# Two-layer decoder kernel: the memory norm's factors per token, and a new order of five Vector steps

## The reference

```python
def first_block(...):
    h = h + short_conv_mixer(rms_norm(h, a_norm), ...)
    h = h + swiglu(rms_norm(h, f_norm[0]), f_w_gu[0], f_w_down[0])
    k_cmp, v_cmp, k_slc, v_slc, k_win, v_win = shared_kv(h, kv_norm, w_kv, ...)
    h = h + nsa_mixer(rms_norm(h, b_norm), b_w_qg, b_w_o, k_cmp, ...)
    h = h + swiglu(rms_norm(h, f_norm[1]), f_w_gu[1], f_w_down[1])
    return rms_norm(h, final_norm)              # eps 1e-5

def second_block(x, c, ...):
    mod = silu(c) @ w_ada + b_ada               # six vectors of 1024
    h = modulate(rms_norm_2(x, g_mix), sh_m, sc_m)   # eps 1e-6
    x = x + gt_m * token_mixer(h, ...)
    h = modulate(rms_norm_2(x, g_ffn), sh_f, sc_f)
    return x + gt_f * swiglu_2(h, ...)
```

## Time and profile before

| | |
|---|---|
| median of 3 runs | 971.0 us (970.72 to 971.22) |
| profiled execution, its own time | 971.74 us |
| its span | 970.0 us |
| TensorE busy | 954.0 us, 98% |
| Vector busy | 712.9 us, 73% |
| Scalar busy | 488.6 us, 50% |
| POOL busy | 88.0 us, 9% |
| mean granted TensorE clock | 0.996 of full |
| chain that ended last | TensorE 86%, Vector 8%, Scalar 3%, issue 2%, DMA 1% |
| DMA | 186.99 MB, 193 GB/s |

### The profile page before, as it was taken

One profiled execution on the slowest core, in us unless ns is written; L12 is line 12 of the kernel. 1 busy time (PEld: TensorE's weight loads), 2 busy tenths in 40 slices (PEclk: granted clock), 3 DMA queues, 4 the chain that ended last, 5 costly groups with the idle time before them and its releaser, 6 DMA issues.

```text
span 970.0 us, 19340 instructions
## 1 busy us (share of the span) xinstructions
PE 954.0 (98%) x7854; PEld 919.1 (95%) x7854; DVE 712.9 (73%) x1131; ACT 488.6 (50%) x712; POOL 88.0 (9%) x132
## 2 busy tenths in 40 slices
PE   8999999999999999899999999999999999999998
PEld 8999999999999977589999999999999999999998
DVE  5886877777769878968777777698876676565654
ACT  5444644433447557847444433537667555334441
POOL 7000000000000042420000000020000000000000
PEclk9999999999999999999999999999999999999999
DMA  9846848686845762038486868435354357564611
GB/s 265 270 174 217 287 157 301 229 285 199 285 165 161 238 217 89 1 133 298 150 299 229 293 204 286 145 113 181 101 173 150 108 179 258 175 218 134 232 66 44
DMA packets 131533, 186.99 MB, mean 193 GB/s; under 512 B 6289, under 2 KB 102929, under 8 KB 131473
## 3 DMA queue, kind: packets, MB, share of 16 engines
q1 hardware_dynamic: 123984, 159.69, 49.7%
q0 software_dynamic: 6912, 25.17, 7.4%
q10 hardware_dynamic: 576, 1.29, 0.4%
HBM read 185.09 MB, written 1.05 MB: 192 GB/s over the span
## 4 chain that ended last, share of the span: by engine, by line
PE 86%; DVE 8%; ACT 3%; issue 2%; DMA 1%; POOL 1%; DVEq 0%; SPq 0%; ACTq 0%; POOLq 0%
PE ps L1898 43%; PE ps L1976 19%; PE ps L1894 12%; PE ps L1896 4%; DVE g_lo L1174 1%; ACT g_hi L668 1%; DMA g_raw<-in_w_up 1%; PE ps L1946 1%; PE ps L2095 1%; PE ps L2042 1%; DVE rstd L1230 1%; PE ps L2160 1%; DVE ybuf L1194 1%; PE ps L2175 1%; DVE e_even L1541 1%
## 5 line engine op out<-in xcount | busy, mean ns | idle before, releaser
L1898 PE MATMUL ps<-opa_hi,g_hi 128*128 128x256 f32 x864 | 230.1, 287 | 1.3 <-ACT opa_hi L717 1.1
L1898 PE MATMUL ps<-opa_lo,g_hi 128*128 128x256 f32 x864 | 220.8, 283 | 0.0
L1898 PE MATMUL ps<-opa_hi,g_lo 128*128 128x256 f32 x864 | 182.8, 284 | 0.0
L1292 DVE TENSOR_TENSOR g_lo<-g_raw,g_hi 128x2048 fp32r<-128x2048 f32 x54 | 123.8, 2293 | 69.0 <-ACT g_hi L742 69.0
L1898 PEld LDWEIGHTS ps<-opa_hi,g_hi 128*128 128x128 f32 x864 | 166.5, 193 | 4.6 <-issue 4.1
L1898 PEld LDWEIGHTS ps<-opa_lo,g_hi 128*128 128x128 f32 x864 | 162.4, 192 | 0.1
L1976 PE MATMUL ps<-hid_hi,d_hi 128*128 128x256 f32 x528 | 147.8, 280 | 1.8 <-DVE hid_lo L1295 1.7
L1976 PE MATMUL ps<-hid_hi,d_lo 128*128 128x256 f32 x528 | 147.5, 279 | 0.0
L1976 PE MATMUL ps<-hid_lo,d_hi 128*128 128x256 f32 x528 | 147.4, 279 | 0.0
L1174 DVE TENSOR_TENSOR g_lo<-g_raw,g_hi 128x2048 fp32r<-128x2048 f32 x54 | 123.6, 2289 | 30.9 <-ACT g_hi L668 30.5
L1898 PEld LDWEIGHTS ps<-opa_hi,g_lo 128*128 128x128 f32 x864 | 139.8, 193 | 0.0
(11 more groups left out here) (340 smaller groups left out, 1809.4 us busy)
## 6 DMA issues: line engine op xcount, KB each, us to landing
g_raw<-in_f_w_gu SPq DMA_DIRECT2D x44, 1024.0 KB, 8.7
ada_raw<-in_w_ada POOLq DMA_DIRECT2D x48, 512.0 KB, 6.3
d_raw<-in_f_w_down SPq DMA_DIRECT2D x22, 1024.0 KB, 5.1
g_raw<-in_w_in SPq DMA_DIRECT2D x14, 1024.0 KB, 8.3
g_raw<-in_w_gate SPq DMA_DIRECT2D x11, 1024.0 KB, 7.2
g_raw<-in_w_up SPq DMA_DIRECT2D x11, 1024.0 KB, 9.7
d_raw<-in_w_down SPq DMA_DIRECT2D x11, 1024.0 KB, 5.3
g_raw<-in_a_w_in SPq DMA_DIRECT2D x10, 1024.0 KB, 8.3
```

The source lines that it names most:

```text
L1292: dve.tensor_tensor(part_view(g_lo, g0 + r, True), raw_cols(c % 2, r % 2, True), part_view(g_hi, g0 + r, True).bitcast(F32), ALU.subtract) ...
L1898: mm = pe.matmul(pair(b)[:, a, :], wt[:, a * P:(a + 1) * P], xt, **st)
```

## The change

The memory norm's two sums come from one set of products with the squares as weights and `sum_w` (two columns per channel tile: g^2 + 1e-6, and 1) moving. The result has tokens on partitions: two columns for each half of the tokens, in banks 4 and 5. Scalar takes two roots of 128x2, Vector the reciprocals of them, and scales the identity by each token's factor (`diag`, 128x128, one for each half). TensorE multiplies `ones` by it (`spread`), which gives the factor of each token on all partitions, in PSUM. `norm_parts` reads the fused factor from there; Scalar copies the plain one to `rstd` later. Vector's sums of squares go; the split of step `MX + 1` is done in two halves, one of them ahead of the reciprocals. POOL makes `sum_w` for `gain_sq`. The counts of the patterns move to bank 3. Outside the norm: the split of the second down slice goes behind the hidden split of step 0 (feed-forward 0 and 1), the scaling of `gmod` and `q_gain` behind step 3, and the two accumulation pairs behind the splits in steps 0 and 1 of the key/value products.

```diff
--- before.py
+++ after.py
@@ -147,8 +147,10 @@
     qg_lo = sb("qg_lo", [P, KT, 48], F32R, on=over_q)
     over_q.close()
     over_q = ExitStack()
-    gain_sq = sb("gain_sq", [P, KT, P], on=over_q)
-    sb("pad_q", [P, 3 * KT * 48 - KT * P], on=over_q)
+    sum_w = sb("sum_w", [P, KT, 2], on=over_q)
+    r_cols = sb("r_cols", [P, 2, TT], on=over_q)
+    diag = sb("diag", [P, 2, TT, P], on=over_q)
+    sb("pad_q", [P, 3 * KT * 48 - 2 * KT - 2 * TT - 2 * TT * P], on=over_q)
     ctx.push(over_q)
     if_raw = sb("if_raw", [P, KT, 8])
     if_hi = sb("if_hi", [P, KT, 36], F32R)
...
@@ -629,10 +631,10 @@
                 pool.tensor_scalar(bias_h[:, h % 2, :], dist[:, :], SLOPES[h], None, ALU.mult).then_inc(bias_made, 1)
         if last_stage >= 5:
 
-            for k in range(KT):
-                g = par_col("final_norm", k)
-                const(pool.tensor_scalar(gain_sq[:, k, :], ones[:, :], g, g, ALU.mult, ALU.mult))
-            const(pool.tensor_scalar(gain_sq[:, :, :], gain_sq[:, :, :], 1e-6, None, ALU.add))
+            g = par_col("final_norm", 0, KT)
+            const(pool.memset(sum_w[:, :, 1], 1.0))
+            const(pool.tensor_tensor(sum_w[:, :, 0], g, g, ALU.mult))
+            const(pool.tensor_scalar(sum_w[:, :, 0], sum_w[:, :, 0], 1e-6, None, ALU.add))
             assert made[0] == c_gain
             const(pool.memset(comb[:, :, :], 0.0))
             for i, r in ((0, 4), (1, 16)):
...
@@ -932,11 +934,13 @@
             for j in range(4):
                 squares(4, j)
 
-            act.wait_ge(ss_done, 5)
-            act.activation(r_next, ps[:, 0, 0:T], ACT.Sqrt, scale=1.0 / D, bias=eps[:, 2:3]).then_inc(rms_made, 1)
+            act.wait_ge(ss_done, 6)
+            for n, e in ((0, 2), (1, 0)):
+                act.activation(r_cols[:, n, :], ps[:, 4:6, n], ACT.Sqrt, scale=1.0 / D,
+                               bias=eps[:, e:e + 1]).then_inc(rms_made, 1)
             hi_of_y([(opa_hi, opa_hi_made, Y_BASE[5], 0)])
-            act.wait_ge(ss_done, 6)
-            act.activation(rstd[:, :], ps[:, 4, 0:T], ACT.Sqrt, scale=1.0 / D, bias=eps[:, 0:1]).then_inc(rms_made, 1)
+            act.wait_ge(r_spread, 2)
+            act.activation(rstd[:, :], ps[:, 1, P:P + T], ACT.Copy).then_inc(rstd_copied, 1)
 
             def evac_values(s):
...
@@ -1187,6 +1191,16 @@
             dve.tensor_tensor(part_view(g_lo, g, paired)[:, 4:8], raw_step(g)[:, 4:8],
                               part_view(g_hi, g, paired)[:, 4:8].bitcast(F32), ALU.subtract).then_inc(g_lo_made, 1)
 
+        def split_half(g, half):
+
+            k = slice(4 * half, 4 * half + 4)
+            paired = CHUNKS[CHUNK_OF[g]][0] == "pair"
+            dve.wait_ge(g_hi_made, g + 1)
+            ins = dve.tensor_tensor(part_view(g_lo, g, paired)[:, k], raw_step(g)[:, k],
+                                    part_view(g_hi, g, paired)[:, k].bitcast(F32), ALU.subtract)
+            if half:
+                ins.then_inc(g_lo_made, 1)
+
         def add_squares(n, pieces=(1, 2, 3)):
 
             for j in pieces:
...
@@ -1297,6 +1311,8 @@
                 c = dc0 + r // 2
                 if not ahead or f == 2:
                     split_d(r % 2, c % 2, s4 + (d0 + r + 1), r % 2)
+                elif r == 0:
+                    split_d(1, c % 2, d0 + 2, 1)
                 if tail and r == 0:
                     split_g(g0 + 22)
                 elif ahead and r == 0:
...
@@ -1307,16 +1323,15 @@
 
             split_g(g0 + 2)
             if f < 2:
-                for r in range(2):
-                    split_d(r, dc0 % 2, d0 + r + 1, r)
+                split_d(0, dc0 % 2, d0 + 1, 0)
             invert_rms(norm)
+            for r in range(4):
+                step(0, r, ahead=r < 2)
             if f == 1:
 
                 dve.wait_ge(mod_made, 1)
                 own(dve.tensor_tensor(gmod[:, 0:8], gmod[:, 0:8], par_col("final_norm", 0, 8), ALU.mult))
                 own(dve.tensor_scalar(q_gain, par_col("q_norm_g_2"), HD ** -0.5, None, ALU.mult))
-            for r in range(4):
-                step(0, r, ahead=r < 2)
             with dve.Fori(1, 5) as i:
                 for r in range(4):
                     step(i, r)
...
@@ -1437,8 +1452,6 @@
             dve.memset(x_cmp[:, :, :, 256:288], 0.0).then_inc(pad_made, 1)
             dve.memset(x_cmp[HD:P, :, :, 255:256], 0.0).then_inc(pad_made, 1)
             split_g(KV + 2)
-            ada_pair(0, 5, 0)
-            ada_pair(0, 5, 1)
             invert_rms(2)
             split_g(KV + 3)
             r_both = rstd[:, :].unsqueeze(1).to_broadcast([P, 2, T])
...
@@ -1482,6 +1495,7 @@
                     gained_lo(s, opb_hi, opb_lo, opb_hi_made, B_FILL["b"], opb_made, "b_norm")
                 if s < 2:
                     split_g(KV + s + 4)
+                    ada_pair(0, 5, s)
                 if s == 4:
                     dve.wait_ge(cmp_hid_done, 1)
                     cmp_blocks(1)
...
@@ -1605,18 +1619,16 @@
         if last_stage >= 5:
 
 
-            total = gu[:, 1, :, :]
-            for j in range(1, 4):
-                dve.wait_ge(sq_made, 4 * 4 + j + 1)
-                ins = dve.tensor_tensor(total, ybuf[:, 0:2, :] if j == 1 else total, ybuf[:, 2 * j:2 * j + 2, :], ALU.add)
-                if j < 3:
-                    own(ins)
-                else:
-                    ins.then_inc(sq_added, 1)
-            dve.wait_ge(rms_made, 5)
-            own(dve.reciprocal(r_next, r_next))
-            norm_parts(r_next, [fill_a("n5", lambda k: gmod[:, k:k + 1], 0)])
-            split_g(MX + 1)
+            split_half(MX + 1, 0)
+            for n in range(2):
+                dve.wait_ge(rms_made, 5 + n)
+                own(dve.reciprocal(r_cols[:, n, :], r_cols[:, n, :]))
+                for a in range(TT):
+                    dve.tensor_scalar(diag[:, n, a, :], ident[:, :], r_cols[:, n, a:a + 1], None,
+                                      ALU.mult).then_inc(diag_made, 1)
+            dve.wait_ge(r_spread, 1)
+            norm_parts(ps[:, 0, P:P + T], [fill_a("n5", lambda k: gmod[:, k:k + 1], 0)])
+            split_half(MX + 1, 1)
             ada_pair(1, 5, 0)
             ada_pair(1, 5, 1)
...
@@ -1716,9 +1728,8 @@
 
             evac_heads(0)
             dve.wait_ge(comb_done, 1)
-            dve.tensor_copy(dil_count[:, :], ps[:, 1, 0:384]).then_inc(comb_done, 1)
-            dve.wait_ge(rms_made, 6)
-            own(dve.reciprocal(rstd[:, :], rstd[:, :]))
+            dve.tensor_copy(dil_count[:, :], ps[:, 3, 0:384]).then_inc(comb_done, 1)
+            dve.wait_ge(rstd_copied, 1)
             split_g(MX + 2)
             scale_residual(0)
...
@@ -1924,7 +1935,7 @@
 
         def sum_squares(n):
 
-            pe.wait_ge(sq_added, norm_index(n) + 1)
+            pe.wait_ge(sq_added, n + 1 if n < 4 else 5)
             parts = 1 if n < 4 else 2
             for k in range(parts):
                 mm = pe.matmul(ps[:, 0, 0:T], ones[:, :], ybuf[:, k, :], start=(k == 0), stop=(k == parts - 1))
...
@@ -1951,12 +1962,17 @@
             for j in range(4):
                 pe.wait_ge(sq_made, 4 * 4 + j + 1)
                 for k in (2 * j, 2 * j + 1):
-                    mm = pe.matmul(ps[:, 0, 0:T], gain_sq[:, k, :], ybuf[:, k, :], start=(k == 0), stop=(k == KT - 1))
-            mm.then_inc(ss_done, 1)
-            pe.wait_ge(sq_added, 5)
-            for k in range(2):
-                mm = pe.matmul(ps[:, 4, 0:T], ones[:, :], gu[:, 1, k, :], start=(k == 0), stop=(k == 1))
-            mm.then_inc(ss_done, 1)
+                    for a in range(TT):
+                        mm = pe.matmul(ps[:, 4 + a, 0:2], ybuf[:, k, a * P:(a + 1) * P], sum_w[:, k, :],
+                                       start=(k == 0), stop=(k == KT - 1))
+            mm.then_inc(ss_done, 2)
+
+        def spread(n):
+
+            pe.wait_ge(diag_made, 2 * n + 2)
+            for a in range(TT):
+                mm = pe.matmul(ps[:, n, P + a * P:2 * P + a * P], ones[:, :], diag[:, n, a, :], start=True, stop=True)
+            mm.then_inc(r_spread, 1)
 
         def ffn(f, norm, hi, lo, ready, hi_ready):
             g0, d0 = FFNS[f], FT * f
...
@@ -2262,13 +2278,15 @@
             pe.wait_ge(consts, c_comb)
             for a, lo, w in ((1, 0, 256), (0, 256, 128)):
                 for i, r in ((0, 4), (1, 16)):
-                    mm = pe.matmul(ps[:, 1, lo:lo + w], comb[0:r, i, a * P:(a + 1) * P], comb[0:r, i, 0:w],
+                    mm = pe.matmul(ps[:, 3, lo:lo + w], comb[0:r, i, a * P:(a + 1) * P], comb[0:r, i, 0:w],
                                    start=(i == 0), stop=(i == 1))
-            mm.then_inc(comb_done, 1)
+                if a == 0:
+                    mm.then_inc(comb_done, 1)
+                spread(1 - a)
 
             def gate_inputs():
 
-                pe.wait_ge(rms_made, 6)
+                pe.wait_ge(rstd_copied, 1)
                 for k in range(KT):
```

(3 more changed lines are left out.)

1 line of the change is left out of this document (added).

## The result

| | before | after |
|---|---|---|
| median | 971.11 us (4 runs, 970.72 to 972.61) | 981.06 us (4 runs, 980.78 to 983.04) |
| ratio, 95% interval | 1 | 1.0105 (1.0091 to 1.0119) |
| span of the profiled execution | 970.0 us | 979.0 us |
| TensorE busy | 954.0 us | 963.2 us |

A forecast was written before the change was run, and what follows sets the result against it. TensorE, busy nearly all the span, was taken as the bound, with gains only where it waits between stages. -0.5 - 1.0 + 1.3 - 0.6 + 0 = -0.8 us, giving 970.2 us from the median of 971.0; range 968.3 to 972.3.

The forecast's parts named there:

- Inside the three feed-forward loops it never waits: Feed-forward loops: TensorE has no waits there, so savings on Vector or Scalar gain nothing; only stage boundaries count.
- First seam: Start of the first feed-forward: moving one down split starts the down products at 121.58 instead of 122.20; net -0.5 us.
- Second seam: Start of the second feed-forward: moving the down split and two small gain operations brings TensorE's next product forward; -1.0 us.
- Key/value stage: Shared key/value products: moved modulation pairs make a modulation load meet the query-weight load, delaying the query product; +1.3 us.
- its ends: Bounds on the key/value cost: +0.15 us if the modulation load starts too late to meet the query load, and +1.6.
- The price of 1.2: Key/value stage: one modulation load costs a weight load in flight 1.2 us, starting 4.7 us after its issue.
- Memory norm: Memory norm: sums end as before, then 1.74 us to the first scaled tile instead of 2.3; -0.6 us.
- The clock: Half-clock dip behind the memory norm: might come sooner or last longer; taken as 0, ends -1.5 and +1.5 us.
- The rival "the clock": Half clock over dense matmuls at the query product and twice 3.4 us at the norm: +3.0, 973.2 us; chance 0.06.
- The narrow products nearly free: Memory norm: sum records at 25 ns each, so sums end with the last square; 968.5 us, chance 0.07.

The follow-up runs named there:

- the seams alone: The kernel before with only the feed-forward reordering: second down split behind step 0's hidden split, gmod and q_gain scaling behind step 3; 970.26 us, ratio 0.9990.
- at equal addresses: The whole change with its last filler tile 16 bytes shorter, so later tiles begin where they did before the change; 974.07 us, ratio 1.0027 to before.
- with 64 columns: The change with addresses of before, modulation products back in their old place, and the norm's sum products widened from 2 to 64 columns; 969.65 us, ratio 0.9989.
- the norm alone: The kernel before with only the memory norm's new two-column form, at the addresses of before; 973.25 us, ratio 1.0010.
- the full layout with the new seams: The kernel before with the feed-forward reordering and tiles placed so loop weights and moving operands begin 64 bytes apart modulo 128; 956.88 us, ratio 0.9868.

## Why the prediction was wrong

The loss adds up from the runs, each kernel against the one it differs from, with before as timed beside it: addresses 981.06 - 974.07 = 7.0, modulation products 974.07 - 971.04 = 3.0, norm 973.25 - 971.78 = 1.5, seams 970.26 - 971.78 = -1.5, together 10.0 us. Measured: 981.06 - 971.11 = 9.95. Each term is good to a microsecond at best: before itself had medians from 971.1 to 971.8 us in the series, and the norm and the seams alone are at the edge of what their runs can tell from nothing. That the sum comes within 0.1 us is luck; the addresses and the modulation products are clear of the noise.

- **"Inside the three feed-forward loops it never waits, so whatever is taken off Vector or Scalar there is worth nothing."** This is the step that failed. It is true of waits, and the prediction took it to mean that nothing in the loops can change. Its sum had no term for what the declarations in the diff do to the products' own time: 7.0 us. The change replaced one tile by three and shortened a filler; the sizes looked equal, 1152 columns for 1152, and rounding made them differ. It is the largest part of the miss and not all of it: at equal addresses the change still takes 974.07 us, above the range's 972.3, by the load and the clock (below).
- **First seam, -0.5**: right, 0.49 with the seams alone, the down products at 121.54 for a forecast of 121.58. That they match to 0.04 us is luck: the kernels drift apart by some tenths before the seam, and in the changed kernel they start at 121.90.
- **Second seam, -1.0**: right, 0.96.
- **Key/value stage, +1.3**: the mechanism was right and the size off. It measured 2.6 at the query product, outside its ends of 0.15 and 1.6. The price of 1.2 came from one weight load that met a modulation load (4.4 us behind its issue at 437.63 by the rows, not 4.7, which changes nothing). Here SP issued the next 2 MB (`in_cmp_w_v`) 1 us sooner as well, at 327.05 at equal addresses where it had been at 328.07, and three loads were on their way before the query weights had landed. The move and this earlier issue were never taken apart, so what the modulation load alone costs stays open.
- **Memory norm, -0.6**: the records were right (3.47 us for a forecast of 3.4), and at one half-clock stretch, with 64 columns, the stage is 0.45 shorter than before. That the sum products can be this narrow at no price to the clock was wrong. The expected 1.74 us from the sums to the first scaled tile were 2.7 in the changed kernel (641.15 to 643.87), at half clock, and 1.8 with 64 columns.
- **The clock, 0**: wrong. The prediction saw that the dip could "be longer" and took the middle. The two-column norm ran with 6.8 us or more at 1.2 GHz in all six profiles that have it, the old norm with 3.4 or none. The rival "the clock" came true as it was written, below 1 behind 337 and for more than 3.4 us behind 636, and its 3.0 us were near: 1.5 at the query product, of which the attention gave 0.6 back, and 1.5 for the norm alone. It had a chance of 0.06, since the prediction held the wait of over 2 us before the query product and the thin work in the norm for weak signs. With it and the load's true size the forecast would have been 974.5 (970.2 + 3.0 + 1.3), near the 974.07 measured at equal addresses.
- **The narrow products nearly free** (25 ns each by the rule of the Trainium skill, "TensorE: Matmul & The Clock Gate", section "Back-to-back issue gap"): the runs decide against it here. The same section says that its formula leaves out the loading of weights and so comes out low for few columns. Two columns and 64 columns both took 0.11 us a record (3.47 and 3.52 us for 32), and each record loads its own 128x128 fp32 weight, shown with 192 ns.

## What to carry to other kernels

When the tiles of a kernel are declared one behind another, treat every changed size as an edit to all that follows: compare the begin of each operand before and after, modulo 256 to be safe, and pin it with a filler. Try weight and moving operand 64 bytes apart where a loop of fp32r products is the bound; one unused tile of 64 bytes gave 0.7% here, the full layout with the new seams 1.3%. And if short products are made for their small cost, look at the granted clock of the dense ones behind; if a wider form costs the same record, try it.

## What the runs showed of the hardware

- An fp32r product of 128x128 weights by 256 columns starts 0.1200 us after the last when both operands begin at the same place modulo 128 (and 256), and after 0.1133 (5.44 us for 48) to 0.1198 (5.75) when they are apart. No wait shows in the profile at any of these paces.
- The mean granted clock tells the kernel before's runs apart: of the 72 timed beside the experiments 11 at 1.000 had a median of 969.5 us, 30 at 0.998 had 971.0, and 29 at 0.996 had 972.1. One stretch of 3.4 us at half clock takes 0.002 off the mean of a span of 970 us, so it costs 1.1 to 1.6 us here.
- From the loop's end to the gate inputs behind the norm: 14.44 us with one such stretch in the old form; 15.3 with two and 16.76 with three in the new one, 13.99 with one and 64 columns.
